# Block input tables of an S5 layer loaded ahead, one block input a step, scans in more and smaller steps

## The chip, the cores and the metric

One NeuronCore of one Trainium2 chip. The metric is the device time of one launch in microseconds. The kernel before takes 2320.91 us, the median of 3 runs (2318.3 to 2321.55).

## The reference

One inference step of a two-layer streaming encoder on two groups of rows at once: a prompt of 512 frames and a running stream of 64 frames, model width 1024. Layer 0 mixes in time with an S5 state-space mixer, layer 1 with differential attention over shared keys and values. Each layer has two SwiGLU feed-forward blocks around its mixer and a LayerNorm after each of the three.

```python
x = layer_norm(ALPHA * x + 0.5 * swiglu(x, w_in[l, 0], w_out[l, 0]), g[0], b[0])
y = s5_mixer(x, ...) if l < N_A else diff_attention(x, ...)
x = layer_norm(ALPHA * x + y, g[1], b[1])
x = layer_norm(ALPHA * x + 0.5 * swiglu(x, w_in[l, 1], w_out[l, 1]), g[2], b[2])
```

The change touches only the S5 mixer. It is a linear recurrence with complex diagonal states, 64 groups of 64 states, followed by a projection to the outputs:

```python
bu = einsum('gpc,btgc->btgp', bb, u_blk)              # complex, bb from the discretised parameters
hs = associative_scan(h[t] = lam_bar * h[t-1] + bu[t])
y_blk = einsum('gcp,btgp->btgc', c_re, hs_re) - einsum('gcp,btgp->btgc', c_im, hs_im)
y = y_blk + d_skip * u                                # then gelu, w_glu, a gated output
```

## The kernel before

All activations stay on the chip, transposed: 8 tiles of 128 features by 576 columns. The columns are worked in two halves, half 0 with 256 and half 1 with 320 (the last 64 of them the running stream). TensorE goes through one long list of weight tiles, 128 outputs by 8 (or 7) rows of 128 inputs. A tile's weights come in float32 from memory into `raw` (four buffers, issued by SyncE), ScalarE rounds them to `wh` (L509), VectorE writes the remainder `wl` (L515), three buffers each, and TensorE does three matmuls for each row (L537 to L539). A feed-forward block has 68 tiles (60 where its last part is held back), in the order gate tile, inner tile and so on, then output tiles.

Everything else is written as generators that are advanced one step after each tile, on each engine by itself: `together` runs several side by side, `chained` one after the other, `idle(n)` skips n steps, and `paced(work, n)` gives work exactly n steps. Engines meet only at semaphores. `packed(work, room)` puts the instructions of a generator into steps: each instruction reports a size, and a step ends when the sizes reach the room; the excess is taken over to the next.

The S5 mixer of a half runs beside a feed-forward block of the other half: `dve_s5`, `act_s5`, `pe_s5` and `pool_s5` of half 0 beside block (0, 1), of half 1 beside block (1, 0), each after the 12 steps of a LayerNorm. Its time axis is cut into blocks of 4 frames. Its steps, counted from 0 at its own start, are these:

- Steps 0 to 5: VectorE and ScalarE rearrange the inputs into `u4` (L1491).
- Block inputs, 8 of them (`dt`): `pe_s5` multiplies `u4` by a table `wt2` of 512 KB (L1711), dt at step 4 + 2 dt, into two banks of `misc` that alternate; ScalarE copies the result into `hs` a step later (L1633), and issues the load of table dt + 2 into the buffer that was just read, as there are two buffers. On every second dt it also issues the loads of an output table `cp2` (512 KB) and `tt2` (256 KB), which have four buffers.
- Two scans, one for each group of four dt, on VectorE alone: `dve_scan` goes up and down a tree over the blocks (L1533 to L1544) with 56 instructions (half 0) or 61 (half 1), of which the widest have 1024 or 1280 elements a partition. `SCAN` is the number of steps of a scan, 11 and 15 for the two halves, and `SCAN_ROOM` its room, 1800 and 1620. The first scan begins at step 11, the second SCAN steps later.
- Outputs: `outputs_at(h, grp)` is the step at which TensorE waits for the scan of a group and begins its four output steps (L1728 and L1731): 23 and 34 for half 0, 27 and 42 for half 1. Four steps later VectorE (L1496) and ScalarE copy them out, and ScalarE applies the GELU.

At the very end the last norm of half 1 is worked out on VectorE in rows and stored by SyncE (L2591). TensorE, which has nothing left to do then, runs the 90 matmuls of `FILL` (L2920 to L2924) on old data into a bank that nobody reads.

Of the kernel before, what the change touches and what calls it, by code (L numbers as in the profile page):

```python
# [15 lines left out]
P = 128  # L16
D = 1024
DT = D // P
# [70 lines left out]
def _ffn(f, h, held=False):  # L89

    for p in range(len(PARTS)):
# [39 lines left out]
BUSY_NORMS = {(0, 1): 10, (2, 1): 5, (3, 1): 4}  # L131
FILL = ((256, 0, 0), (320, 0, 0), (288, 0, 0), (512, 0, 0), (384, 0, 0), (320, 32, 0), (288, 32, 0), (320, 4, 0), (304, 0, 0),
        (320, 0, 16), (320, 16, 0), (448, 0, 0), (256, 32, 0), (320, 0, 4), (272, 0, 0), (320, 0, 32), (192, 0, 0), (320, 8, 0))

# [96 lines left out]
def build(nc, x_prompt, x_sample, cache_k, cache_v, state_re, state_im, ln_g, ln_b, w_in, w_out,  # L231
# [4 lines left out]
    with ctx:  # L236

        def sem(name):
            return ctx.enter_context(nc.semaphore(name))
# [1224 lines left out]
        s_u4a = sem("u4_ready_act")  # L1464
        s_wl = [sem(f"wt2_loaded{s}") for s in range(2)]
        s_bl = [sem(f"cp2_tt2_loaded{s}") for s in range(4)]
# [12 lines left out]

        SCAN = (11, 15)  # L1480
        INPUTS = 4

        def outputs_at(h, grp):
            return 12 + (grp + 1) * SCAN[h]

# [105 lines left out]
        def dve_s5(dve, h):  # L1591
            scans = chained(idle(11), paced(packed(dve_scan(dve, h, 0), SCAN_ROOM[h]), SCAN[h]),
                            paced(packed(dve_scan(dve, h, 1), SCAN_ROOM[h]), SCAN[h]))
            return paced(together(dve_u4(dve, h), scans,
                                  chained(idle(outputs_at(h, 0) + 4), dve_y(dve, h, 0)),
                                  chained(idle(outputs_at(h, 1) + 4), dve_y(dve, h, 1))), s5_steps(h))

        SCAN_ROOM = (1800, 1620)

# [11 lines left out]
        def act_load_inputs(act, h, dt):  # L1611
            n = DT * h + dt
            wait(act, s_wm, n - 1)
            act.dma_start(wt2[dt % 2][:].rearrange("p a q s -> p (a q s)"), scr_w[dt]).then_inc(s_wl[dt % 2], 16)

        def act_load_outputs(act, h, dt):
            n = DT * h + dt
            wait(act, s_ym, n - 3)
            act.dma_start(cp2[dt % 4][:].rearrange("p a q n -> p (a q n)"), scr_c[dt]).then_inc(s_bl[dt % 4], 16)
            act.dma_start(tt2[dt % 4][:].rearrange("p q n -> p (q n)"), scr_t[dt]).then_inc(s_bl[dt % 4], 16)  # L1620

        def act_block_inputs(act, h):
            n, G = NBLK[h], NGRP[h]
            tables_stored(act)
            act_load_inputs(act, h, 0)
            act_load_inputs(act, h, 1)
            yield from idle(INPUTS + 1)
            for dt in range(DT):
                act.wait_ge(s_wm, DT * h + dt + 1)
                if dt == 0 and h:  # L1630
                    act.wait_ge(s_ym, DT)
                for ri in range(2):
                    nc.scalar.copy(hs[:, dt // 4, 0:G, 1:GB + 1, ri, 4 * (dt % 4):4 * (dt % 4) + 4],  # L1633
                                   misc[:, 2 * (dt % 2) + ri, 0:4 * n].rearrange("p (q g i) -> p g i q", q=4, i=GB)
                                   ).then_inc(s_wc, 1)
                if dt + 2 < DT:
                    act_load_inputs(act, h, dt + 2)
                yield
                if dt % 2 == 0:
                    act_load_outputs(act, h, dt // 2)  # L1640
                yield
# [53 lines left out]
        def pe_s5(pe, h):  # L1695
            n = NBLK[h]
            yield from idle(INPUTS)
            for dt in range(DT):
                s = dt % 2
                if dt % 4 == 0:  # L1700
                    pe.wait_ge(s_u4d, len(U4_DVE) * (2 * h + dt // 4 + 1))
                    pe.wait_ge(s_u4a, len(U4_ACT) * (2 * h + dt // 4 + 1))
                if dt == 0 and h:
                    pe.wait_ge(s_yd, 2 * len(Y_DVE))
                    pe.wait_ge(s_ya, 2 * len(Y_ACT))
                pe.wait_ge(s_wl[s], 16 * (DT // 2 * h + dt // 2 + 1))
                if dt >= 2:
                    pe.wait_ge(s_wc, 2 * (DT * h + dt - 1))
                for ri in range(2):
                    for q in range(4):  # L1710
                        mm = nc.tensor.matmul(misc[:, 2 * s + ri, q * n:(q + 1) * n], wt2[s][:, ri, q, :],  # L1711
                                              u4[:, dt, q, 0:n], start=True, stop=True, skip_group_check=True)
                mm.then_inc(s_wm, 1)
                yield from idle(2)
            at = INPUTS + 2 * DT
            for grp in range(2):
# [922 lines left out]
        def _(act):  # L2639
# [23 lines left out]
            finish(beside)  # L2663
            beside = chained(act_ln(act, 0, 1), act_s5(act, 1))
            ffn(1, 0, beside)
# [190 lines left out]
        def _(pe):  # L2856
# [62 lines left out]
            finish(beside)  # L2919
            for cols, at, w_at in FILL:  # L2920
                for j in range(5):
                    w, x = wh[j % 2][:].rearrange("p k c -> p (k c)"), (hh, hl)[j % 2][:].rearrange("p k n -> p (k n)")
                    nc.tensor.matmul(ps[:, 0, 0:cols], w[:, w_at:w_at + P], x[:, at:at + cols],  # L2923
                                     start=True, stop=True, skip_group_check=True)  # L2924

# [40 lines left out]
```

## Time and profile before

| | |
|---|---|
| median of 3 runs | 2320.91 us (2318.3 to 2321.55) |
| the profiled execution | 2318.73 us, span of its instructions 2316.9 us |
| TensorE busy, matmuls | 2257.6 us, 97% of the span |
| VectorE busy | 1525.1 us, 66% |
| ScalarE busy | 1144.4 us, 49% |
| GpSimd busy | 575.2 us, 25% |
| loaded from memory | 366.53 MB, 168 GB/s over the span with what is written |
| mean granted TensorE clock | 0.996 |

The span is what the instructions of the profiled execution cover; the time has a little around it. A share is an average over stages, so an engine with 66% can be the one that is late in a stage. PE is TensorE, PEld its weight load, DVE VectorE, ACT ScalarE, POOL GpSimd, SP SyncE, and a q behind the name its queue. A line number of a weight tile is that of a helper, so stages are told apart by their time: the S5 steps of half 0 run from about 285 us, those of half 1 from about 605 us.

### The profile page before, as it was taken

To read this page: it belongs to the slowest core of one execution; us is meant where nothing else is said; L and a number is where in the kernel's file an instruction comes from. 1 tells how busy PE (TensorE), PEld (TensorE's weight loads), DVE (VectorE), ACT (ScalarE), POOL (GpSimd) and SP (SyncE) were. 2 spreads that over 40 slices of the span, in tenths; PEclk is the share of its full clock that TensorE was granted. 3 is DMA by queue.
4 is the path that set the end of the run, shared out by engine and by line. 5 is a ranking of instruction groups with operands and counts; after the bars stand their busy time and mean duration, and the time that the engine had idled before them with its cause. 6 is when DMAs were issued, how large, how long until landed. Compare 5 with 4: busy or idle time off the path is not lost.

```text
span 2316.9 us, 42849 instructions
## 1 busy us (share of the span) xinstructions
PE 2257.6 (97%) x17261; PEld 2217.1 (96%) x17261; DVE 1525.1 (66%) x2292; ACT 1144.4 (49%) x1923; POOL 575.2 (25%) x491
## 2 busy tenths in 40 slices
PE   8989999999998998999999999999999999999999
PEld 8989999999998998999999999999999998999999
DVE  6898768657788578444475575656677665475444
ACT  4434543555645546433365465555466564354332
POOL 2267401123211343111251123010352011132110
PEclk9999999999999999999999999999999999999999
DMA  9568675454765455655569656544556456355452
GB/s 251 168 194 234 191 217 181 123 171 137 218 216 172 138 162 148 183 151 147 151 191 291 189 160 178 154 122 134 148 154 189 135 147 190 115 152 170 143 156 80
DMA packets 705367, 391.15 MB, mean 169 GB/s; under 512 B 25001, under 2 KB 693138, under 8 KB 705170
## 3 DMA queue, kind: packets, MB, share of 16 engines
q1 hardware_dynamic: 662720, 332.44, 49.6%
q10 hardware_dynamic: 42450, 55.96, 7.3%
q8 instruction: 138, 2.26, 0.4%
q14 instruction: 59, 0.48, 0.1%
HBM read 366.53 MB, written 21.82 MB: 168 GB/s over the span
## 4 chain that ended last, share of the span: by engine, by line
PE 75%; DVE 9%; ACT 2%; issue 2%; POOL 1%; ACTq 0%; POOLq 0%; DVEq 0%
PE tile_ps L537 22%; PE tile_ps L539 22%; PE tile_ps L538 22%; DVE wl L515 3%; PE misc L1731 1%; PE misc L1711 1%; ACT wh L509 1%; PE misc L2064 1%; PE misc L2089 1%; POOL zq L870 1%; PE misc L2264 1%; DVE r L828 1%; DVE hs L1539 1%; PE tile_ps L2923 1%; PE misc L1728 1%
## 5 line engine op out<-in xcount | busy, mean ns | idle before, releaser
L515 DVE TENSOR_TENSOR wl<-raw,wh 128x1024 fp32r<-128x1024 f32 (+1 forms) x640 | 796.6, 1245 | 444.2 <-ACT wh L509 442.3
L537 PE MATMUL tile_ps<-xh,wh 128*128 128x256 f32 (+1 forms) x3520 | 1051.9, 299 | 21.4 <-DVE wl L515 16.9
L539 PE MATMUL tile_ps<-xh,wl 128*128 128x256 f32 (+1 forms) x3520 | 1035.5, 294 | 0.0
L538 PE MATMUL tile_ps<-xl,wh 128*128 128x256 f32 (+1 forms) x3520 | 1035.4, 294 | 0.0
L509 ACT CAST wh<-raw 128x1024 fp32r<-128x1024 f32 (+1 forms) x640 | 655.0, 1025 | 734.0 <-PE tile_ps L539 723.3
L537 PEld LDWEIGHTS tile_ps<-xh,wh 128*128 128x128 f32 x3520 | 666.1, 189 | 29.5 <-issue 18.7
L538 PEld LDWEIGHTS tile_ps<-xl,wh 128*128 128x128 f32 x3520 | 666.1, 189 | 0.9
L539 PEld LDWEIGHTS tile_ps<-xh,wl 128*128 128x128 f32 x3520 | 665.9, 189 | 0.0
L725 POOL TENSOR_TENSOR hl<-hf,hh 128x256 fp32r<-128x256 f32 (+1 forms) x176 | 243.7, 1384 | 1269.8 <-ACT hh L633 1269.2
L537 PE MATMUL tile_ps<-hh,wh 128*128 128x320 f32 (+1 forms) x1472 | 441.9, 300 | 5.4 <-DVE wl L515 5.1
L538 PE MATMUL tile_ps<-hl,wh 128*128 128x320 f32 (+1 forms) x1472 | 433.0, 294 | 0.0
L539 PE MATMUL tile_ps<-hh,wl 128*128 128x320 f32 (+1 forms) x1472 | 432.8, 294 | 0.0
L537 PEld LDWEIGHTS tile_ps<-hh,wh 128*128 128x128 f32 x1472 | 276.9, 188 | 9.5 <-issue 7.5
L538 PEld LDWEIGHTS tile_ps<-hl,wh 128*128 128x128 f32 x1472 | 277.0, 188 | 0.3
L539 PEld LDWEIGHTS tile_ps<-hh,wl 128*128 128x128 f32 x1472 | 276.8, 188 | 0.0
L698 DVE SCALAR_TENSOR_TENSOR r<-r,tile_ps 128x256 f32<-128x256 f32 (+1 forms) x208 | 94.0, 452 | 142.8 <-PE tile_ps L539 141.5
L627 ACT ACTIVATE sil<-tile_ps 128x320 f32<-128x320 f32 (+1 forms) x140 | 57.6, 412 | 179.6 <-PE tile_ps L539 177.8
L675 DVE SCALAR_TENSOR_TENSOR hf<-sil,tile_ps 128x256 f32<-128x256 f32 (+1 forms) x176 | 79.4, 451 | 79.3 <-PE tile_ps L539 77.0
L633 ACT CAST hh<-hf 128x256 fp32r<-128x256 f32 (+1 forms) x176 | 75.7, 430 | 69.8 <-DVE hf L675 68.2
L764 POOL TENSOR_TENSOR zc<-zc,r 128x256 f32<-128x256 f32 (+1 forms) x64 | 65.3, 1020 | 123.3 <-DVE r L698 76.5
L890 POOL TENSOR_TENSOR xl<-r,xh 128x256 fp32r<-128x256 f32 (+1 forms) x60 | 68.8, 1165 | 91.3 <-ACT xh L803 52.6
L870 POOL TENSOR_TENSOR zq<-zq,sq 128x256 f32<-128x256 f32 (+1 forms) x54 | 61.7, 1142 | 17.5 <-ACT sq L798 11.6
(303 smaller groups left out, 1803.4 us busy)
## 6 DMA issues: line engine op xcount, KB each, us to landing
raw<-in_ffn_w_in_dram SPq DMA_DIRECT2D x352, 512.0 KB, 3.8
raw<-in_ffn_w_out_dram SPq DMA_DIRECT2D x128, 448.0 KB, 3.7
raw<-in_ffn_w_out_dram SPq DMA_DIRECT2D x64, 512.0 KB, 4.0
raw<-in_ssm_w_glu_dram SPq DMA_DIRECT2D x32, 512.0 KB, 3.8
raw<-in_attn_w_kv_dram SPq DMA_DIRECT2D x32, 512.0 KB, 4.0
wt<-scr_w ACTq DMA_DIRECT2D x16, 512.0 KB, 4.7
cp<-scr_c ACTq DMA_DIRECT2D x16, 512.0 KB, 4.3
raw<-in_attn_w_q_dram SPq DMA_DIRECT2D x16, 512.0 KB, 3.9
```

What stands on the lines that cost most here:

```text
L509: nc.scalar.copy(wh[n % WS][:, 0:k, :], raw[n % RAWS][:, 0:k, :]).then_inc(w_hi, 1)
L515: nc.vector.tensor_tensor(wl[n % WS][:, 0:k, :], raw[n % RAWS][:, 0:k, :], wh[n % WS][:, 0:k, :].bitcast(F32), ALU.subtract).then_inc(w_lo, 1)
L537: nc.tensor.matmul(o, wh[w][:, kk, :], xa, start=kk == 0, stop=False)
L538: nc.tensor.matmul(o, wh[w][:, kk, :], xb, start=False, stop=False)
L539: return nc.tensor.matmul(o, wl[w][:, kk, :], xa, start=False, stop=kk == ROWS[n] - 1)
L633: nc.scalar.copy(hh[:, i, 0:N], hf[:, 0:N]).then_inc(hh_ready, 1)
L675: nc.vector.scalar_tensor_tensor(out=hf[:, 0:N], in0=sil[:, 0:N], scalar=0.25 if (f, h, p) in TANH else 0.5, in1=bank(n + 1, h), op0=ALU.m ...
L698: nc.vector.scalar_tensor_tensor(out=r[:, d, CS[h]], in0=r[:, d, CS[h]], scalar=alpha, in1=bank(n, h), op0=ALU.mult, op1=ALU.add).then_inc ...
L725: nc.gpsimd.tensor_tensor(hl[:, i, 0:N], hf[:, 0:N], hh[:, i, 0:N].bitcast(F32), ALU.subtract).then_inc(hl_ready, 1)
L764: nc.gpsimd.tensor_tensor(zc[:, 0:N], zc[:, 0:N], r[:, d, CS[h]], ALU.add).then_inc(ln_zc, 1)
L870: nc.gpsimd.tensor_tensor(zq[:, 0:N], zq[:, 0:N], sq[d % 3][:, 0:N], ALU.add).then_inc(ln_zq, 1)
L890: nc.gpsimd.tensor_tensor(low[:, d, 0:NT[h]], r[:, d, CS[h]], high[:, d, 0:NT[h]].bitcast(F32), ALU.subtract).then_inc(x_ready[h], 1)
```

## The change

1. Six block input tables are on chip at a time instead of two: two in `wt2` and four in the buffers of the output tables `cp2`, which have the same size (`input_table`). In half 0 they are loaded in steps 0 to 4, in half 1 in the first steps of the feed-forward block before the norm (`act_inputs_ahead`). Tables 6 and 7 go into `wt2` once block inputs 0 and 1 are multiplied.
2. A block input is multiplied in each step from 4 to 11, instead of in every second one from 4 to 18.
3. The output tables of group 0 are loaded at steps 13, 15, 17 and 19, once the buffers are free of input tables.
4. The scans begin at step 8 instead of 11, and have 13 and 12 steps in half 0, 17 and 16 in half 1, with rooms of 1490, 1620, 1400 and 1490. `outputs_at` gives 22 and 34 for half 0, 26 and 42 for half 1. The S5 work has as many steps in all as before, 47 and 55.
5. The `FILL` matmuls at the end are left out.

```diff
--- before.py
+++ after.py
@@ -129,8 +129,6 @@
 BUSY_TILES = {FIRST["in", 3, 1, 0]: 5}
 BUSY_ROWS = {FIRST["in", 1, 0, 0]: 4, FIRST["o", 1]: 8}
 BUSY_NORMS = {(0, 1): 10, (2, 1): 5, (3, 1): 4}
-FILL = ((256, 0, 0), (320, 0, 0), (288, 0, 0), (512, 0, 0), (384, 0, 0), (320, 32, 0), (288, 32, 0), (320, 4, 0), (304, 0, 0),
-        (320, 0, 16), (320, 16, 0), (448, 0, 0), (256, 32, 0), (320, 0, 4), (272, 0, 0), (320, 0, 32), (192, 0, 0), (320, 8, 0))
 
 HID = {}
 for _f in range(4):
@@ -1462,7 +1460,7 @@
 
         s_u4d = sem("u4_ready_dve")
         s_u4a = sem("u4_ready_act")
-        s_wl = [sem(f"wt2_loaded{s}") for s in range(2)]
+        s_wl = [sem(f"block_input_table_loaded{b}") for b in range(6)]
         s_bl = [sem(f"cp2_tt2_loaded{s}") for s in range(4)]
         s_wm = sem("block_inputs_multiplied")
         s_wc = sem("block_inputs_copied")
@@ -1477,11 +1475,17 @@
         s_so = sem("states_copied")
 
 
-        SCAN = (11, 15)
+        SCAN = ((13, 12), (17, 16))
         INPUTS = 4
+        SCAN_AT = INPUTS + 4
 
         def outputs_at(h, grp):
-            return 12 + (grp + 1) * SCAN[h]
+            return SCAN_AT + 1 + sum(SCAN[h][:grp + 1])
+
+        def input_table(h, dt):
+            b = dt % 6
+            table = wt2[b] if b < 2 else cp2[b - 2]
+            return table, s_wl[b], 16 * (2 * h + 1 + dt // 6 if b < 2 else h + 1)
 
         def s5_steps(h):
             return outputs_at(h, 1) + 13
@@ -1589,13 +1593,13 @@
                 yield
 
         def dve_s5(dve, h):
-            scans = chained(idle(11), paced(packed(dve_scan(dve, h, 0), SCAN_ROOM[h]), SCAN[h]),
-                            paced(packed(dve_scan(dve, h, 1), SCAN_ROOM[h]), SCAN[h]))
+            scans = chained(idle(SCAN_AT), paced(packed(dve_scan(dve, h, 0), SCAN_ROOM[h][0]), SCAN[h][0]),
+                            paced(packed(dve_scan(dve, h, 1), SCAN_ROOM[h][1]), SCAN[h][1]))
             return paced(together(dve_u4(dve, h), scans,
                                   chained(idle(outputs_at(h, 0) + 4), dve_y(dve, h, 0)),
                                   chained(idle(outputs_at(h, 1) + 4), dve_y(dve, h, 1))), s5_steps(h))
 
-        SCAN_ROOM = (1800, 1620)
+        SCAN_ROOM = ((1490, 1620), (1400, 1490))
 
         def act_u4(act, h):
             tables_stored(act)
@@ -1609,22 +1613,28 @@
                         yield
 
         def act_load_inputs(act, h, dt):
-            n = DT * h + dt
-            wait(act, s_wm, n - 1)
-            act.dma_start(wt2[dt % 2][:].rearrange("p a q s -> p (a q s)"), scr_w[dt]).then_inc(s_wl[dt % 2], 16)
+            table, loaded, _ = input_table(h, dt)
+            wait(act, s_wm, DT * h + dt - 5 if dt >= 6 else DT * h)
+            wait(act, s_ym, DT * h)
+            act.dma_start(table[:].rearrange("p a q s -> p (a q s)"), scr_w[dt]).then_inc(loaded, 16)
 
         def act_load_outputs(act, h, dt):
             n = DT * h + dt
+            act.wait_ge(s_wm, DT * h + min(dt + 3, DT))
             wait(act, s_ym, n - 3)
             act.dma_start(cp2[dt % 4][:].rearrange("p a q n -> p (a q n)"), scr_c[dt]).then_inc(s_bl[dt % 4], 16)
             act.dma_start(tt2[dt % 4][:].rearrange("p q n -> p (q n)"), scr_t[dt]).then_inc(s_bl[dt % 4], 16)
 
         def act_block_inputs(act, h):
             n, G = NBLK[h], NGRP[h]
-            tables_stored(act)
-            act_load_inputs(act, h, 0)
-            act_load_inputs(act, h, 1)
-            yield from idle(INPUTS + 1)
+            if h == 0:
+                tables_stored(act)
+                act_load_inputs(act, h, 0)
+                for dt in range(1, INPUTS + 2):
+                    act_load_inputs(act, h, dt)
+                    yield
+            else:
+                yield from idle(INPUTS + 1)
             for dt in range(DT):
                 act.wait_ge(s_wm, DT * h + dt + 1)
                 if dt == 0 and h:
@@ -1633,11 +1643,18 @@
                     nc.scalar.copy(hs[:, dt // 4, 0:G, 1:GB + 1, ri, 4 * (dt % 4):4 * (dt % 4) + 4],
                                    misc[:, 2 * (dt % 2) + ri, 0:4 * n].rearrange("p (q g i) -> p g i q", q=4, i=GB)
                                    ).then_inc(s_wc, 1)
-                if dt + 2 < DT:
-                    act_load_inputs(act, h, dt + 2)
-                yield
-                if dt % 2 == 0:
-                    act_load_outputs(act, h, dt // 2)
+                if dt < 2:
+                    act_load_inputs(act, h, dt + 6)
+                yield
+            for dt in range(4):
+                act_load_outputs(act, h, dt)
+                yield
+                yield
+
+        def act_inputs_ahead(act):
+            for dt in range(6):
+                act_load_inputs(act, 1, dt)
+                yield
                 yield
 
         def act_y(act, h, grp):
@@ -1697,22 +1714,23 @@
             yield from idle(INPUTS)
             for dt in range(DT):
                 s = dt % 2
+                table, loaded, count = input_table(h, dt)
                 if dt % 4 == 0:
                     pe.wait_ge(s_u4d, len(U4_DVE) * (2 * h + dt // 4 + 1))
                     pe.wait_ge(s_u4a, len(U4_ACT) * (2 * h + dt // 4 + 1))
                 if dt == 0 and h:
                     pe.wait_ge(s_yd, 2 * len(Y_DVE))
                     pe.wait_ge(s_ya, 2 * len(Y_ACT))
-                pe.wait_ge(s_wl[s], 16 * (DT // 2 * h + dt // 2 + 1))
+                pe.wait_ge(loaded, count)
                 if dt >= 2:
                     pe.wait_ge(s_wc, 2 * (DT * h + dt - 1))
                 for ri in range(2):
                     for q in range(4):
-                        mm = nc.tensor.matmul(misc[:, 2 * s + ri, q * n:(q + 1) * n], wt2[s][:, ri, q, :],
+                        mm = nc.tensor.matmul(misc[:, 2 * s + ri, q * n:(q + 1) * n], table[:, ri, q, :],
                                               u4[:, dt, q, 0:n], start=True, stop=True, skip_group_check=True)
                 mm.then_inc(s_wm, 1)
-                yield from idle(2)
-            at = INPUTS + 2 * DT
+                yield
+            at = INPUTS + DT
             for grp in range(2):
                 yield from idle(outputs_at(h, grp) - at)
                 at = outputs_at(h, grp) + 4
@@ -2661,7 +2679,7 @@
             beside = act_ln_quick(act, 1, 0)
             act_out(act, 0, 1, 2, beside)
             finish(beside)
-            beside = chained(act_ln(act, 0, 1), act_s5(act, 1))
+            beside = together(act_inputs_ahead(act), chained(act_ln(act, 0, 1), act_s5(act, 1)))
             ffn(1, 0, beside)
             finish(beside)
             act.dma_start(cosT[:, :], rope_cos).then_inc(s_cs, 16)
@@ -2917,11 +2935,6 @@
             beside = together(chained(pe_ln(pe, 5, 0), pe_y_a(pe)), chained(idle(Y_LAST + 2), pe_y_b(pe)))
             ffn(3, 1, beside)
             finish(beside)
-            for cols, at, w_at in FILL:
-                for j in range(5):
-                    w, x = wh[j % 2][:].rearrange("p k c -> p (k c)"), (hh, hl)[j % 2][:].rearrange("p k n -> p (k n)")
-                    nc.tensor.matmul(ps[:, 0, 0:cols], w[:, w_at:w_at + P], x[:, at:at + cols],
-                                     start=True, stop=True, skip_group_check=True)
 
 
 def rope_tables():
```

## Rows read from the trace of the kernel before

**Rows 1.** The page: busy time by engine, and the chain that ended last by line.

```profile
PE 2257.6 (97%) x17261; PEld 2217.1 (96%) x17261; DVE 1525.1 (66%) x2292; ACT 1144.4 (49%) x1923; POOL 575.2 (25%) x491
...
PE tile_ps L537 22%; PE tile_ps L539 22%; PE tile_ps L538 22%; DVE wl L515 3%; PE misc L1731 1%; PE misc L1711 1%; ACT wh L509 1%; PE misc L2064 1%; PE misc L2089 1%; POOL zq L870 1%; PE misc L2264 1%; DVE r L828 1%; DVE hs L1539 1%; PE tile_ps L2923 1%; PE misc L1728 1%
```

**Rows 2.** Waits of TensorE, 370 to 435 us: in total, times, longest.

```profile
PE tile_ps L537 <- DVE wl L515: 2.0, 2, 1.4
PE misc L1728 <- DVE hs L1544: 1.7, 1, 1.7
```

**Rows 3.** Waits of TensorE, 640 to 700 us.

```profile
PE tile_ps L537 <- DVE wl L515: 1.1, 2, 0.9
PE misc L1728 <- DVE hs L1544: 0.6, 1, 0.6
```

**Rows 4.** Waits of TensorE, 700 to 765 us.

```profile
PE tile_ps L537 <- DVE wl L515: 7.0, 5, 2.7
PE misc L1728 <- DVE hs L1544: 0.4, 1, 0.4
```

**Rows 5.** Stretches: length, busy PE, PEld, DVE, ACT, POOL (counts), clock, DMA share, GB/s.

```profile
626.70:646.70 20.00, 20.00 (x173) 20.00 (x173) 9.38 (x12) 7.19 (x11) 0.00 (x0) 1.00 0.89 272
646.70:699.10 52.40, 50.64 (x429) 49.87 (x427) 50.16 (x91) 22.54 (x38) 9.01 (x7) 1.00 0.63 201
699.10:721.20 22.10, 22.05 (x182) 22.05 (x183) 17.07 (x23) 3.30 (x4) 0.00 (x0) 1.00 0.77 238
721.20:761.40 40.20, 33.13 (x252) 32.10 (x251) 38.35 (x75) 26.60 (x36) 9.86 (x7) 0.92 0.47 138
```

**Rows 6.** Timeline of VectorE: start, us, operation [idle before it, releaser].

```profile
638.13 1.23 DVE L515 TENSOR_TENSOR wl<-raw,wh 128x1024 fp32r<-128x1024 f32 x1 [0.71 <-ACT wh L509]
...
647.07 1.49 DVE L1533 TENSOR_TENSOR sa<-hs,lam 128x1280 f32<-128x1280 f32 x1
648.48 0.82 DVE L1535 TENSOR_TENSOR sb<-hs,lam 128x640 f32<-128x640 f32 x1
...
650.68 0.82 DVE L1537 TENSOR_TENSOR sb<-hs,lam 128x640 f32<-128x640 f32 x1
651.53 1.49 DVE L1539 TENSOR_TENSOR hs<-hs,sa 128x1280 f32<-128x1280 f32 x1
653.06 0.42 DVE L698 SCALAR_TENSOR_TENSOR r<-r,tile_ps 128x256 f32<-128x256 f32 x1
653.40 1.22 DVE L515 TENSOR_TENSOR wl<-raw,wh 128x1024 fp32r<-128x1024 f32 x1
654.53 2.02 DVE L1542 TENSOR_TENSOR hs<-hs,sb 128x1280 f32<-128x1280 f32 x1
```

**Rows 7.** Timeline of TensorE around two block inputs and the first outputs.

```profile
624.74 1.91 PE L1711 MATMUL misc<-u,wt 128*128 128x80 f32 x16
626.44 0.36 PE L537 MATMUL tile_ps<-hh,wh 128*128 128x256 f32 x1
...
632.18 1.91 PE L1711 MATMUL misc<-u,wt 128*128 128x80 f32 x16
...
699.15 0.45 PE L1728 MATMUL misc<-u,tt 128*128 128x80 f32 x2 [0.61 <-DVE hs L1544]
```

**Rows 8.** The end: closing matmuls (ns min/median/max), VectorE's last row, its stores.

```profile
L2923 PE MATMUL tile_ps<-hh,wh x54: 250/308/393, 2302.1 to 2315.3; 128*128 128x320 f32 x24, 128*128 128x256 f32 x6, 128*128 128x288 f32 x6, 128*128 128x512 f32 x3
...
2312.11 1.28 DVE L2575 SCALAR_TENSOR_TENSOR yrow<-yrow,ysd,brow 64x1024 f32<-64x1024 f32 x1
...
out_dram<-yrow SPq DMA_DIRECT2D x1, 256.0 KB, 2.9
```

**Rows 9.** The page, DMA issues: KB each, median us from issue to landing.

```profile
wt<-scr_w ACTq DMA_DIRECT2D x16, 512.0 KB, 4.7
```

**Rows 10.** Stretches: length, busy PE, granted clock, DMA share, GB/s.

```profile
734.00:735.00 1.00, 0.99 (x9) 1.00 1.02 301
738.00:742.00 4.00, 4.00 (x24) 0.57 0.47 131
```

## The prediction, made before the changed kernel ran

> **What bounds the kernel now.** I read the page first. TensorE is busy for 97% of the span, and the chain that ended last is the three matmul lines of the weight tiles, 22% each [rows 1]. So time can be won or lost only where TensorE waits, and where instructions are added to or taken from it. Then I read the waits of TensorE alone in the three stretches that the change touches. While the S5 work of half 0 runs, TensorE waits 2.0 us for weight remainders (`wl`, written by VectorE) and 1.7 us for a finished scan [rows 2]: 3.7 us. For the first scan of half 1 it is 1.1 + 0.6 us [rows 3], for the second 7.0 + 0.4 us [rows 4]: 9.1 us. All of it is VectorE being late; no wait for a table load stands in these answers. The stretches by engine say why: from 646.7 to 699.1 VectorE is busy 50.16 of 52.40 us, from 721.2 to 761.4 38.35 of 40.20, but from 626.7 to 646.7, while the first block inputs are multiplied, only 9.38 of 20.00 [rows 5]. So the bound in these stages is VectorE, and the question is what the new step plan does to the moment at which each scan ends and to the moment at which TensorE asks for it.
>
> **Numbers of one step (half 1).** A weight tile of 8 rows takes (632.18 - 624.74 - 1.70)/2 = 2.87 us on TensorE, 1.70 being the 16 matmuls of a block input: the next weight matmul starts that long after the first of them [rows 7]; a tile of 7 rows 7/8 of it, 2.51. VectorE owes each step 0.34 us (residual add, start to start) and 1.13 us (`wl`), 1.48 together [rows 6], 1.34 with 7 rows. Scan instructions, start to start: 1280 elements 1.41 us, 1.53 when linked to the one before; 640 elements linked 0.85; in general elements/960 + 0.08, or + 0.20 if linked. About one in two steps loses a further 0.53 us: the third 1280-element row starts after a `wl` and takes 2.02 where its twin takes 1.49 [rows 6].
>
> **Scan packing, from the code.** A scan of half 1 has 61 instructions with sizes that sum to 23,740. Room 1620 packs them into 14 batches: 2040, 2040, 1340, 1080, 1780, 1580, 1496, 1804, 1540, 1840, 1780, 1340, 1400, 2680. They start at S5 step 11, so the last falls on step 24 of 11 to 25, and TensorE asks at step 27. Room 1400 makes 17 batches: 2040, 2040, 1340, 700, 1460, 1080, 1200, 1372, ..., the last 1340 on step 24 of 8 to 24; TensorE asks at step 26. Group 1: before 26 to 39, asked at 42; after 16 batches (room 1490) on 25 to 40, asked at 42. So three earlier steps are gained at the front, yet the last batch has the same VectorE step (24) or a later one (39 to 40), and its margin to the asking step falls from three steps to two. The totals of steps do not change (47 and 55), nor does any instruction of the S5 work.
>
> **Group 0 of half 1.** VectorE does the same work up to the end of step 24 in both kernels, so the scan ends later or sooner only by the difference in VectorE's idle time. Before: 10.6 us idle in 626.7 to 646.7, and of the 2.24 us not busy until 699.1 I take 1.0 as waits, the rest as gaps between instructions: 11.6 [rows 5]. After: each of the steps 4 to 11 carries a block input, 2.87 + 1.70 = 4.57 us of TensorE. The tile of step 6 ends 1.70 later than now, at 626.44; the `wl` of step 8 is done 2 x 4.57 + 2.26 after it (0.42 + 0.71 wait for ScalarE + 1.13 [rows 6]), at 637.8. From 626.4 that is 11.4 us less three steps of 1.48: 7.0 idle. Steps 8 to 11 give VectorE 4 x 4.57 = 18.3 us for 4 x 1.48 and four batches, 2.5 + 2.4 + 1.5 + 0.75 = 7.2: 5.2 idle. Sum 12.2 against 11.6, so the scan ends where it does now, +-1 us. But it is asked for one tile earlier. Now TensorE has finished the tile of step 27 at 698.5 and waits 0.6; after, it has that tile still to do when the scan ends, and waits instead. It is one tile behind: **+2.9 us** (bounds +1.5 and +4). Where a stall goes, the later one takes its place: the waits for `wl` shrink or grow, the sum to that point is VectorE's.
>
> **Group 1 of half 1.** Before, VectorE has caught up at 721.2 (step 31) and is then full to the scan's end at 761.4, 40.2 us [rows 5]. After, it catches up last at step 30, because the four output steps, 22.1 us for four tiles [rows 5], now lie at 26 to 29. From there it owes the same plus two steps' own work (1.34 + 1.34, steps 30 and 40) and 700 elements of size that were done earlier before (0.75 us): 3.4 us more, from a start 2.51 us sooner. VectorE's four `ysb` copies lie one step earlier and inside both sums. **+0.9 us** (bounds 0 and +2).
>
> **Half 0.** FFN columns are 320 here, tiles longer, margins to the asking step two and two in both kernels (last batches at 21/32 asked at 23/34; after 20/32, asked at 22/34). What changes is group 1: by step 27 the sizes done sum to 11,592 against 10,900, so about 690 elements, 0.7 us, less remain behind the same deadline. **-0.7 us** of the 3.7 waited (bounds -2 and 0). The final batches (1656, 1656, 1084) are the same, so the 1.7 us wait for the scan stays.
>
> **Loads and queues.** The same 48 loads move the same bytes. In half 1 six input tables move to steps 0 to 10 of the feed-forward ahead, past the first norm; ScalarE's instructions behind them wait for nothing, as the counts that they ask for (all block inputs and outputs of half 0) were reached a stage before. In half 0 six tables of 512 KB in five steps of 3.5 us stand beside one weight tile of 512 KB each: 11 x 0.524 MB in 17.7 us, 326 GB/s, above the 301 GB/s of a full microsecond [rows 10]. The excess, 0.4 MB, is 1.5 us of queue. A table lands in 4.7 us [rows 9] and is issued three steps, 10 us, before it is multiplied; a weight tile is issued some three tiles ahead. Hidden: 0, and up to +3 if not. The Trainium skill ("DMA: Bandwidth & Descriptors", on issuing engines not being separate DMA queues) says that loads issued by different engines run on the same 16 engines and interleave, which speaks against bunching them; taken alone it would put the 1.5 us into the weight tiles' landing, which the sum leaves hidden. Output tables of 4 dts are issued at steps 13 to 19 instead of 6 to 18 and are needed from 22 or 26: hidden. Block inputs in successive steps need ScalarE's two copies within one step of 4.57 us, beside 1.05 of cast: hidden.
>
> **The 90 closing matmuls.** They run from 2302.1 to 2315.6 and write a buffer that nobody reads [rows 8]. They look like the end of the chain [rows 1], but VectorE's last row goes to 2313.4 and its store takes 2.9 us more, 2316.3 of a span of 2316.9 [rows 8]. The store is the cover: the end moves by 0 (bounds -0.7 and 0).
>
> **The sum.** +2.9 + 0.9 - 0.7 + 0 = +3.1 us on the profiled execution's 2318.73 (span 2316.9 and 1.8 around it): 2321.8. The median of the runs shown is 2320.91, 2.2 us above it; on it the forecast is 2324.0.
>
> **Rivals.** (A) The lighter steps do relieve VectorE: 1400 to 1490 of size per step are 0.14 to 0.23 us less than 1620, over 12 steps 2 to 3 us that TensorE would not wait, and if the idle time at the front is really used, most of the 12.8 us goes, with the slow clock in it: -6, 2315. For it: three more steps. Against it: the packing above, whose sizes done by steps 35 to 38 are equal to the unit (16,540 to 21,060), and 12.2 us idle that stays. 0.14. (B) Slower by more: the new waits sit together ahead of an output step and the clock falls over it. Now the granted clock is 1.00 before the two waits of 2.7 and 2.0 us in 735 to 751 but 0.57 over 738 to 742, a fall to 1.2 GHz after the first, which is 4 x 0.43 = 1.7 us of work lost [rows 10]; there most of it is hidden, since VectorE binds. After group 0 of half 1 nothing hides it: the four output steps are TensorE's. One such there, and one later beside another norm, give +3.1 + 1.7 + 1.7 = +6.5, 2327.4. It decides once TensorE's wait at the asking step reaches about the 2.7 us seen. The Trainium skill ("TensorE: Matmul & The Clock Gate", Part 1) calls the gate free-running, not reset by the kernel; by that, which waits are hit would vary from run to run, and the same plan could give +3 or +6. 0.26. (C) The step plan is shifted but nothing is late enough to matter, within 1 us of now: 2321.5. This lies inside my range and shares its class. 0.10.
>
> **Numbers.** The forecast has 0.50. A measurement of this kernel can tell about 0.2% (4.6 us) from no change, so +3.1 is within it. Same: most of the forecast and of C, and a little of A and B: 0.59. Slower: most of B and the upper end of the forecast (+4.6 is 1.5 above it): 0.27. Faster: A, 0.14. Range: from -4 (the low half of A left out) to +7.5: 2317 to 2328.5.
>
> **What would show it.** Right: the wait of the first output matmul of half 1 for its scan grows from 0.6 us towards 2, the waits before it sum to about 4 with it instead of 1.7; those of the second scan to about 8; the scan of group 0 ends at the same distance from the last `u4` copy; half 0 loses under 1 us of its 3.7; VectorE stays near half idle in steps 6 to 8; the end is a store. Wrong: VectorE busy through the block inputs, waits under 5 us in half 1, a wait for `wh` on a load, or a span that shrinks by the closing matmuls.

## The result, and the profile after

The changed kernel takes 2329.82 us, the median of 6 runs (2326.86 to 2331.74), against 2320.93 (2318.3 to 2322.8): a ratio of 1.0037, 95% interval 1.0027 to 1.0047. It is slower, where the forecast was 2324.0 with a change too small to tell from none. The profiled execution took 2331.31 us, in the upper part of its kernel's runs, with a span of 2329.5; that is 12.6 us over the one of before, so its pieces add up to more than the 8.9 us between the medians.

The page of the changed kernel, busy time and the chain that ended last (compare [rows 1]; the lines have moved by two, L535 to L537 are the weight tiles, and L1746 and L1749 the output matmuls):

```profile
PE 2252.4 (97%) x17171; PEld 2210.4 (95%) x17171; DVE 1524.7 (65%) x2292; ACT 1144.0 (49%) x1923; POOL 573.7 (25%) x491
...
PE 71%; DVE 8%; issue 6%; POOL 3%; ACT 2%; ACTq 0%; POOLq 0%; DVEq 0%
```

TensorE is busy 5 us less, as the closing matmuls are gone, yet the span grew. The kernel before without its closing matmuls (the first run below) is busy for 2242.5 us with the same 17171 instructions: so the same matmuls took 9.9 us longer here. The waits of TensorE (total us, times, longest), first for 370 to 435 us, then 640 to 706, then 706 to 775, answer to [rows 2 to 4]:

```profile
PE misc L1746 <- DVE hs L1548: 2.1, 1, 2.1
PE tile_ps L535 <- DVE wl L513: 2.0, 3, 1.0
...
PE tile_ps L535 <- DVE wl L513: 2.1, 3, 1.1
PE misc L1746 <- DVE hs L1548: 1.8, 1, 1.8
...
PE tile_ps L535 <- DVE wl L513: 7.0, 5, 2.1
PE misc L1746 <- DVE hs L1548: 0.6, 1, 0.6
```

Half 0 waits 4.1 us (3.7 before), half 1 11.5 (9.1): +2.8 us of waits. That is close to what the forecast said of the sum of waits, +3.1. Most of the rest stands in the granted clock. Stretches of the changed kernel (length, busy of PE, PEld, DVE, ACT and POOL, clock, DMA share, GB/s):

```profile
626.00:646.00 20.00, 20.00 (x176) 20.00 (x176) 12.62 (x22) 10.08 (x17) 0.00 (x0) 1.00 0.62 186
646.00:705.30 59.30, 55.23 (x464) 53.82 (x463) 53.08 (x93) 25.23 (x40) 7.78 (x7) 1.00 0.65 194
433.60:443.80 10.20, 10.20 (x46) 10.20 (x45) 2.52 (x3) 0.00 (x0) 0.00 (x0) 0.52 0.50 143
706.70:713.50 6.80, 6.80 (x35) 6.80 (x34) 5.73 (x9) 0.00 (x0) 0.00 (x0) 0.53 0.48 137
```

And the same place in half 0 of the kernel before:

```profile
433.00:444.00 11.00, 11.00 (x87) 11.00 (x86) 3.07 (x4) 3.36 (x5) 1.82 (x2) 1.00 0.50 144
```

TensorE is busy in both, but gets through 46 instructions in 10.2 us where it got through 87 in 11.0: 1.2 GHz instead of 2.4. Right ahead of each slow stretch it had waited for a scan, as the timeline of TensorE shows (start, us, idle before in brackets). The third line is of the weight tile behind the first output step of half 0: it runs slow as well.

```profile
433.11 0.62 PE L1746 MATMUL misc<-u,tt 128*128 128x64 f32 x2 [2.08 <-DVE hs L1548]
433.52 1.06 PE L1749 MATMUL misc<-hs,cp 128*128 128x64 f32 x4
...
439.13 0.47 PE L535 MATMUL tile_ps<-hh,wh 128*128 128x320 f32 x1
...
705.25 0.45 PE L1746 MATMUL misc<-u,tt 128*128 128x80 f32 x2 [1.77 <-DVE hs L1548]
```

At these two places 10.2 x 0.48 = 4.9 and 6.8 x 0.47 = 3.2 us of work were lost; the kernel before lost nothing at either (1.00 in the line above, and 1.00 over 699.10 to 721.20 in [rows 5]). By landmarks (the same matmul in both traces), the profiled executions differ by 1.4 us before the S5 steps begin, by 0.6 more at the first output of the second scan of half 0, by 4.8 more at the norm after that stage, by 5.4 more at the second scan of half 1, and by 0.4 more in all that follows. The 1.4 us is there before any changed step runs, and nothing here explains it; in other profiles below this difference is up to 4.3 us. At the end VectorE and the store still close the kernel:

```profile
2322.30 4.21 SPq L2609 DMA_DIRECT2D out_dram<-yrow  x3
...
2324.69 1.28 DVE L2593 SCALAR_TENSOR_TENSOR yrow<-yrow,ysd,brow 64x1024 f32<-64x1024 f32 x1
```

### The profile page after: what moved, and what is told of

The parts are those of the page before. It is cut to its first block, busy times and chain, and to the rows that moved or that the text cites. A ratio compares the mean times of both kernels' runs of the same rounds, so it can differ in the third digit from the quotient of the medians.

```text
span 2329.5 us, 42689 instructions
## 1 busy us (share of the span) xinstructions
PE 2252.4 (97%) x17171; PEld 2210.4 (95%) x17171; DVE 1524.7 (65%) x2292; ACT 1144.0 (49%) x1923; POOL 573.7 (25%) x491
## 4 chain that ended last, share of the span: by engine, by line
PE 71%; DVE 8%; issue 6%; POOL 3%; ACT 2%; ACTq 0%; POOLq 0%; DVEq 0%
PE tile_ps L535 21%; PE tile_ps L537 21%; PE tile_ps L536 21%; DVE wl L513 2%; PE misc L1749 2%; POOL zq L868 1%; PE misc L2082 1%; ACT wh L507 1%; PE misc L2107 1%; POOL hl L723 1%; PE misc L2282 1%; PE misc L1746 1%; PE misc L1729 1%; DVE r L826 1%; DVE hs L1543 0%
## 5 line engine op out<-in xcount | busy, mean ns | idle before, releaser
L535 PE MATMUL tile_ps<-xh,wh 128*128 128x256 f32 (+1 forms) x3520 | 1052.3, 299 | 22.0 <-DVE wl L513 17.0
L537 PE MATMUL tile_ps<-xh,wl 128*128 128x256 f32 (+1 forms) x3520 | 1035.1, 294 | 0.0
L535 PEld LDWEIGHTS tile_ps<-xh,wh 128*128 128x128 f32 x3520 | 665.5, 189 | 31.6 <-issue 19.0
L537 PEld LDWEIGHTS tile_ps<-xh,wl 128*128 128x128 f32 x3520 | 665.1, 189 | 0.0
L535 PE MATMUL tile_ps<-hh,wh 128*128 128x320 f32 (+1 forms) x1472 | 443.5, 301 | 5.7 <-DVE wl L513 5.6
L537 PE MATMUL tile_ps<-hh,wl 128*128 128x320 f32 (+1 forms) x1472 | 434.0, 295 | 0.0
L535 PEld LDWEIGHTS tile_ps<-hh,wh 128*128 128x128 f32 x1472 | 278.0, 189 | 10.0 <-issue 8.0
L537 PEld LDWEIGHTS tile_ps<-hh,wl 128*128 128x128 f32 x1472 | 277.7, 189 | 0.0
L868 POOL TENSOR_TENSOR zq<-zq,sq 128x256 f32<-128x256 f32 (+1 forms) x54 | 62.8, 1163 | 17.4 <-ACT sq L796 11.5
```

Source lines behind the costliest of these rows:

```text
L535: nc.tensor.matmul(o, wh[w][:, kk, :], xa, start=kk == 0, stop=False)
L537: return nc.tensor.matmul(o, wl[w][:, kk, :], xa, start=False, stop=kk == ROWS[n] - 1)
L868: nc.gpsimd.tensor_tensor(zq[:, 0:N], zq[:, 0:N], sq[d % 3][:, 0:N], ALU.add).then_inc(ln_zq, 1)
```

## The experiments

The theory: TensorE's waits grow by about 3 us, and the waits of 1.8 and 2.1 us stand just ahead of the output steps, over which the clock then falls. Rivals: waits alone, the loads, the closing matmuls.

**The parts one by one.** The closing matmuls alone:

```diff
-            for cols, at, w_at in FILL:
-                for j in range(5):
...
```

> The kernel before without the 90 closing matmuls and nothing else. Theory 'scans and clock' (the 8.9 us come from the S5 steps): the end is VectorE's last row and its store, so the time stays within 1 us of the kernel before (2320.9). Rival 'closing matmuls' (they matter for a reason that the trace does not show): some of the 8.9 us shows here, 2323 or more, and the span starts or ends otherwise.

2319.7 us, ratio 0.9998 (0.9989 to 1.0006), span 2316.9 as before. The rival is out, and every run below whose edit starts from the changed kernel can be read against the kernel before.

This profile shows one thing more. Its S5 steps are those of the kernel before, yet TensorE waits 10.5 us in half 1, not 9.1. The stretch where the difference arises, first before, then without the closing matmuls:

```profile
750.00:757.00 7.00, 6.11 (x39) 6.14 (x40) 6.96 (x6) 2.93 (x6) 5.10 (x3) 0.76 0.42 124
...
750.00:757.00 7.00, 5.22 (x43) 5.08 (x44) 6.96 (x6) 3.04 (x6) 5.11 (x3) 1.00 0.41 119
```

VectorE is full in both. Where the clock fell, TensorE worked slower and waited less; where it did not, it waited instead. So in the stretch that VectorE bounds a slow clock costs next to nothing, and sums of waits in half 1 can be compared only between profiles with as many slow stretches there. The kernel before and the changed one have two each.

Then the tables ahead and one block input a step, with the old steps for everything else:

```diff
-        SCAN = ((13, 12), (17, 16))
+        SCAN = ((11, 11), (15, 15))
+        OUTPUTS = ((23, 34), (27, 42))
...
-        SCAN_AT = INPUTS + 4
+        SCAN_AT = (11, 11)
...
-            return SCAN_AT + 1 + sum(SCAN[h][:grp + 1])
+            return OUTPUTS[h][grp]
...
-        SCAN_ROOM = ((1490, 1620), (1400, 1490))
+        SCAN_ROOM = ((1800, 1800), (1620, 1620))
```

> Tables loaded ahead and one block input a step, without the closing matmuls, but both scans and the outputs at the steps and rooms of the kernel before (start 11; 11, 11, 15, 15 steps; outputs at 23, 34, 27, 42). Theory 'scans and clock': 2320 to 2323, as no scan moves; waits before the outputs as in the kernel before (1.7, 0.6, 0.4 us), no half clock over the output steps. Rival 'loads' (bunched tables delay weight tiles, or one input a step takes VectorE's time from the first scan): a wait of ScalarE for a load, or 2326 and more.

2331.91 us, 1.0052 (1.0039 to 1.0064): at least as slow as the whole change, whose interval (1.0027 to 1.0047) it overlaps. My theory was that nothing would happen without a moved scan; it is wrong. Waits of TensorE in 370 to 440 us and in 640 to 780, and the stretch behind a new wait of 1.5 us at the first outputs of half 0:

```profile
PE misc L1747 <- DVE hs L1549: 3.2, 2, 1.7
PE tile_ps L535 <- DVE wl L513: 2.0, 2, 1.4
...
PE tile_ps L535 <- DVE wl L513: 15.0, 13, 2.7
PE misc L1747 <- DVE hs L1549: 0.9, 2, 0.6
...
384.70:391.50 6.80, 6.80 (x35) 6.80 (x36) 6.73 (x8) 0.46 (x1) 1.29 (x1) 0.58 0.45 124
```

No wait of TensorE or of ScalarE in these stages is for a load. Whether it is the loads' place or the block inputs' was settled by putting the block inputs back to every second step, and with them ScalarE's copies and the loads of the output tables between them:

```diff
-            for dt in range(4):
-                act_load_outputs(act, h, dt)
-                yield
+                if 2 <= dt < 6:
+                    act_load_outputs(act, h, dt - 2)
...
-                yield
-            at = INPUTS + DT
+                yield from idle(2)
+            at = INPUTS + 2 * DT
```

> Tables loaded ahead, but block inputs in every second step and the scans and outputs as in the kernel before; no closing matmuls. The run with one input a step had 2331.9. Theory 'block inputs leave the first scan' (four of the eight, 6.8 us of TensorE, stood beside the first scan of each half and gave VectorE time): 2319 to 2322, no wait before the first outputs of half 0. Rival 'loads': 2326 or more, as the loads are where they were.

2322.95 us, 1.0000 (0.9991 to 1.0009), 1 us above what the theory gave and far from the rival's 2326, and the waits of half 0 are those of before, with no wait at its first outputs:

```profile
PE tile_ps L535 <- DVE wl L513: 2.0, 2, 1.4
PE misc L1746 <- DVE hs L1549: 1.7, 1, 1.7
...
PE tile_ps L535 <- DVE wl L513: 8.1, 7, 2.6
PE misc L1746 <- DVE hs L1549: 0.8, 2, 0.5
```

So loading the input tables ahead costs and brings nothing. One block input a step, with the copies and output tables that go with it, costs 9 us between the medians of these two runs and 12 by their ratios. The theory names the reason: four of the eight used to stand beside the first scan and gave VectorE 4 x 1.7 us there. The waits fit it: 15.9 us in half 1 against 8.9 with the old block input steps, of which some 3 us stand for two slow stretches that only the second of these profiles has. The 1.7 us beside each step were not varied by themselves. Then, on top of the run with one input a step, the scan steps of one half at a time:

> As the run before, with the changed kernel's scan steps in half 0 alone. Theory 'scans and clock': TensorE's waits change by under 1 us, but the wait for the second scan is about 2.1 us and the granted clock then falls to half over the output steps, 10 us long in the profile of the changed kernel: 2325 to 2327 where it falls. Rival 'waits alone': 2320 to 2322.

> As the second run, with the changed kernel's scan steps in half 1 alone. Theory 'scans and clock': the first scan is asked for one tile earlier, +2 to +3 us by waits, and +3.4 us where the clock falls over its output steps (6.8 us at half): 2323 to 2327. Rival 'waits alone': 2323 to 2324 and the clock at 1.0 over the outputs of group 0.

2327.80 us, 1.0030 (1.0019 to 1.0041), with the new scans of half 0 alone, 2329.62, 1.0044 (1.0030 to 1.0058), with those of half 1 alone. Both lie above what the theory gave, which had counted from about 2321, while the run that they start from took 2331.91. The waits show what each repairs of what one input a step had broken: 4.1 us in half 0 instead of 5.2, and 11.2 in half 1 instead of 15.9, or of 13.0 in the first of the two, which has the same steps there and as many slow stretches. Between the times only the gain of the first is clear of noise, and just so. And the fall of the clock that the theory expected came in neither profile: none behind the wait of 2.1 us at the second outputs of half 0 in the first, none behind the 1.85 us at the first outputs of half 1 in the second. So a wait of that length does not always bring the clock down. The intervals overlap with the changed kernel's, and I do not rank them.

**The clock.** Spare matmuls keep TensorE busy until the scan is there:

```diff
+        BUSY_SCANS = ((0, 9), (8, 3))
...
-                pe.wait_ge(s_sh, 2 * h + grp + 1)
                 pe.wait_ge(s_wc, 2 * DT * (h + 1))
...
+                pe_busy(misc[:, 0, 0:P], BUSY_SCANS[h][grp])
+                pe.wait_ge(s_sh, 2 * h + grp + 1)
```

> The changed kernel, with TensorE kept busy by 9 spare matmuls of ones before it waits for the second scan of half 0, 8 before the first and 3 before the second scan of half 1; they end about when the scan does. Theory 'scans and clock': the granted clock stays at 1.0 over the output steps, which gives back up to the 5.1 and 3.4 us that the profile lost there: 2322 to 2326. Rival 'waits alone': no gain, 2329 to 2331.

2323.87 us, 1.0010 (1.0001 to 1.0018): 6 us less than the changed kernel. The spare matmuls on the timeline of TensorE, and the stretches that were slow (PE alone, then clock):

```profile
431.94 2.17 PE L524 MATMUL misc<-vec,ones 128*128 128x128 f32 x18
434.17 0.43 PE L1749 MATMUL misc<-u,tt 128*128 128x64 f32 x2
...
430.00:446.00 16.00, 15.94 (x125) 1.00 0.57 162
697.00:712.00 15.00, 15.00 (x125) 1.00 0.58 178
```

No work was saved, and VectorE is as late as it was (2.0 and 9.2 us of waits for `wl` against 2.0 and 9.1 in the changed kernel; the waits for the scans are filled by the spare matmuls). Only the clock held at these two places. What is left over the kernel before, 2.5 us, is the waits' share.

The other way round, the kernel before with its second scan of half 0 made later:

```diff
                 else:
+                    if h == 0 and grp == 1:
+                        link(dve, V.tensor_tensor(t1[..., halves[0]], cur[..., halves[1]], lim[..., halves[0]], ALU.mult))
                     V.tensor_tensor(nxt, nxt, t1, ALU.add).then_inc(done, 1)
```

> The kernel before, with the second scan of half 0 made about 0.7 us later by one 512-element product that is done twice with the same result. Theory 'clock': TensorE's wait for that scan goes from 1.7 to about 2.3 us, above the 2.1 of the changed kernel, and the granted clock then often falls over the four output steps, for 3.4 to 10 us: 2323 to 2327. Rival 'waits alone': +0.7, 2321 to 2322.

and with `link(dve, V.tensor_tensor(t0, cur, lre, ALU.mult))` ahead of it as well:

> The same with that scan about 2.0 us later (a 1024-element product as well). Theory 'clock': the wait is about 3.6 us and the clock falls in nearly every run: +2.0 by the wait and +3 to +5 by the clock, 2326 to 2329. Rival 'waits alone': +2.0, 2323.

2324.15 us, 1.0019 (1.0010 to 1.0028), and 2326.83 us, 1.0024 (1.0014 to 1.0033). First the one, then the other, the first output matmul and the stretch behind it:

```profile
433.94 0.43 PE L1730 MATMUL misc<-u,tt 128*128 128x64 f32 x2 [2.79 <-DVE hs L1546]
...
434.00:446.00 12.00, 12.00 (x72) 12.00 (x73) 4.80 (x6) 2.69 (x3) 1.79 (x2) 0.72 0.33 93
```

```profile
436.87 0.48 PE L1731 MATMUL misc<-u,tt 128*128 128x64 f32 x1 [4.46 <-DVE hs L1547]
...
434.50:446.00 11.50, 9.13 (x39) 9.13 (x40) 5.35 (x6) 0.00 (x0) 1.24 (x2) 0.60 0.40 118
```

The waits grew by 1.1 and 2.8 us, more than the 0.7 and 2.0 that I had expected, and the times by 3.6 and 6.3 between the medians (4.4 and 5.6 by the ratios). In both the clock fell behind the wait: 12.0 x 0.28 = 3.4 us of work in the first, three times what the wait had grown by, and 11.5 x 0.40 = 4.6 us in the second, where the wait is 4.46.

**Where the outputs are asked for.** The changed kernel with one step more before the first outputs of half 1:

```diff
+        OUTPUTS = ((22, 34), (27, 42))
...
-            return SCAN_AT + 1 + sum(SCAN[h][:grp + 1])
+            return OUTPUTS[h][grp]
```

> The changed kernel with TensorE asking for the first scan of half 1 at step 27 again instead of 26, nothing else. Theory 'asked a tile earlier': the 1.8 us wait before the first output shrinks to under 0.5 and the clock does not fall over these outputs: 2 to 5 us less than the changed kernel, 2325 to 2328. Rival 'VectorE's order alone' (the sum of the waits is VectorE's and does not care where they stand): within 1 us of 2329.8.

2324.81 us, 1.0012 (1.0003 to 1.0020), 5 us less than the changed kernel, as the theory had it (its range began at 2325). There is no wait before these outputs any more. But the waits of half 1 (640 to 780 us) hardly shrank:

```profile
PE tile_ps L535 <- DVE wl L513: 9.7, 10, 1.9
PE misc L1747 <- DVE hs L1549: 1.4, 1, 1.4
```

11.1 us against 11.5 (all idle time of TensorE there, 11.7 in both): what the first scan no longer costs, waits beside the second one do. A part of that is the clock's: it falls once in the stretch that VectorE bounds, not twice as in the changed kernel, and by the first run a fall there takes 1.4 us off the waits. The gain in time is a scan wait gone from ahead of the first outputs, where in this profile the clock no longer falls (1.00 over 700 to 714 us).

**A version that beats both.** Scans from step 8 as in the change, but with room before each asking step:

```diff
-        SCAN = ((13, 12), (17, 16))
+        SCAN = ((14, 11), (20, 12))
+        OUTPUTS = ((26, 34), (32, 42))
...
-            return SCAN_AT + 1 + sum(SCAN[h][:grp + 1])
+            return OUTPUTS[h][grp]
...
-        SCAN_ROOM = ((1490, 1620), (1400, 1490))
+        SCAN_ROOM = ((1400, 1800), (1300, 1900))
```

> Tables ahead and one input a step, scans from step 8, but 14 and 11 steps in half 0 with outputs at 26 and 34, 20 and 12 in half 1 with outputs at 32 and 42, rooms 1400, 1800, 1300, 1900: four to seven steps between the last batch of the first scan and its outputs. Adding up VectorE's steps by the durations of the trace gives no wait in half 0 and 5 us in half 1, against 4.1 and 11.5 in the changed kernel. Theory 'margins': 2311 to 2317. Rival 'VectorE has simply too much to do': over 2320.

2313.84 us, 0.9967 (0.9955 to 0.9979). Waits in 370 to 440 us and 640 to 780:

```profile
PE misc L1747 <- DVE ysb L1501: 1.7, 1, 1.7
...
PE tile_ps L535 <- DVE wl L513: 4.6, 6, 1.2
PE misc L1747 <- DVE hs L1549: 1.2, 1, 1.2
```

The 1.7 us were not in my sum: the copies of the first outputs were late for the second. With the first outputs of half 0 at 25:

> The run with wide margins (2313.8) with the first outputs of half 0 at 25 instead of 26. There TensorE waited 1.7 us at the second outputs of half 0 for the copies of the first ones. Theory 'copies': one step earlier these copies are in time, and the wait falls below 0.5 us: 2311 to 2313. Rival 'the scan takes their place': VectorE's copies, now beside the same scan a step earlier, leave the scan as late as it was: the wait stays above 1 us, 2313 to 2315.

2312.15 us, 0.9964 (0.9951 to 0.9976), within noise of the run before it. The time would fit the theory (2311 to 2313), but the wait decides: the one for the copies is gone, and one of 1.3 us for the scan has taken its place, as the rival said. Last, the kernel before with nothing but its first outputs later:

```diff
-            return 12 + (grp + 1) * SCAN[h]
+            return ((26, 34), (30, 42))[h][grp]
```

> The kernel before with one line changed: TensorE asks for the first scan's outputs at step 26 instead of 23 in half 0, and at 30 instead of 27 in half 1; tables, block inputs, scans and closing matmuls as they were. Theory 'margins' (what pays is where the four output steps and their copies stand beside the second scan, which is VectorE's tightest stretch, not loading ahead): the waits of half 0 fall from 3.7 to under 2 us, those of half 1 from 9 to 6 or 7: 2313 to 2317, most of what the run with wide margins won. Rival 'the early scans are what pays': 2319 or more.

2314.20 us, 0.9970 (0.9959 to 0.9981). One line gives nearly all of it, without any of the change. Waits in 370 to 440 us and 640 to 780:

```profile
PE misc L1728 <- DVE ysb L1496: 1.7, 1, 1.7
...
PE tile_ps L537 <- DVE wl L515: 4.8, 6, 1.5
PE tile_ps L537 <- issue: 1.7, 1, 1.7
PE misc L1728 <- DVE hs L1544: 1.0, 1, 1.0
```

(The 1.7 us put down to "issue" end at 697.95, as VectorE's `wl` of that tile is done at about 697.9, so they look like a wait for VectorE too.) The waits fell by 3.6 us, the time by 6.4; what the rest is was not taken apart.

The likely reason, worked out from the rows and not tested by itself: the four output steps make TensorE's steps some 3 us longer each (22.10 us [rows 5] less four tiles of 2.51). Beside the start of the second scan VectorE could not use that time: its batches are capped by the room, and it idled (17.07 of 22.10 us busy). Three steps later they stand where its lag is greatest.

## Why the prediction was wrong

- **The bound** was read rightly. VectorE's lateness sets these stages; all waits of TensorE in these stages are on it, none on a load (one of 1.7 us, in the last run, is put down to "issue").
- **Scan packing and margins** held: the last batches fell where the code puts them, and the margin, not the start, is what counts.
- **Group 0 of half 1**: the scan ended where the forecast put it. Last `u4` copies and last scan instruction, before and after:

```profile
624.50 1.85 DVE L1491 COPY u<-r 32x320 f32<-32x320 f32 x4
697.18 1.92 DVE L1544 TENSOR_TENSOR hs<-hs,sb 128x1280 f32<-128x1280 f32 x1
...
630.79 1.84 DVE L1495 COPY u<-r 32x320 f32<-32x320 f32 x4
703.71 1.48 DVE L1548 TENSOR_TENSOR hs<-hs,sb 128x1280 f32<-128x1280 f32 x1
```

  From the end of the copies to the end of the scan it is 72.8 us before and 72.6 after. The idle time of VectorE that stays, 12.2 us, is 7.4 in 626 to 646 and at most 6.2 in 646 to 705.3, about as worked out. The price of +2.9 was too high: the waits there grew by 2.2 (1.7 to 3.9). And its reason is shown only in part: asking at 27 again takes the wait away from these outputs and 5 us off the time, but the sum of the waits of half 1 stays at 11.1, partly because the clock fell once less there.
- **Group 1 of half 1**: +0.9 forecast, +0.2 measured (7.4 to 7.6).
- **Half 0**: -0.7 forecast, +0.4 measured. The waits for `wl` stayed at 2.0 and the one for the scan went from 1.7 to 2.1, where I had said that it stays.
- **Loads and closing matmuls**: nothing, measured apart, as forecast. The tables of half 0 landed in 5.6 to 6.6 us instead of 4.7, still in time.
- **The sum of the waits**, +3.1 forecast, was +2.8. That it came so close is partly luck: the two terms of half 1 were too high by 1.4 together, and that of half 0 was too low by 1.1, with the wrong sign.
- **The step that failed** is the sum itself, which has no term for the clock: it adds up waits and puts nothing beside them. In the stretch that I had read the clock's loss is hidden, as VectorE is the bound, and I left it at that. I had it as rival B, at 0.26, for half 1 alone and with a threshold of 2.7 us that I took from the one wait I had looked at. The fall came in half 1 behind a wait of 1.8 us, and in half 0, which B does not name, behind 2.1. The output steps are TensorE's own time, so nothing hides it. It cost 4.9 + 3.2 us in the profile; by the run with spare matmuls, it is 6 us of the 8.9.
- **A price by chance.** The same wait at the second outputs of half 0 had different sequels. A wait of 1.7 us was followed by a full clock in four profiles (the kernel before, without the closing matmuls, tables ahead, first version with wide margins) and by a slow one in three (one input a step, the same with the scans of half 1, the one-line change). A wait of 2.1 us there was followed by a full clock with the scans of half 0 alone, by 3.4 us of slow clock with the outputs of half 1 asked at 27, and by 10.2 us in the changed kernel. The Trainium skill ("TensorE: Matmul & The Clock Gate", Part 1) says that the window in which TensorE's activity is judged runs free and is not reset when a kernel starts. The profiles fit that, though none shows where such a window lies. I had the sentence, and should have drawn from it that such a wait has a price by chance, and not a point from which it decides.

How often the clock falls at each wait stays open, as each kernel has one profile. But every run has its mean granted clock on record, and these bear the account out beyond the profiles. TensorE idles at the end of every kernel without the closing matmuls, and the clock is at 0.50 there, so these are compared with each other. Without the closing matmuls and nothing else the mean is 0.9930 (11 runs), in the changed kernel 0.9898 (6 runs, the highest 0.991), with the spare matmuls 0.9928 (11 runs). The first difference, 0.0032 of 2328 us, is an estimate of 7.4 us of work lost to the clock, hidden losses included; with the 2.8 us of waits it makes 10.2, against 10.1 between the medians. The later scans lower the mean of the kernel before from 0.9950 (21 runs) to 0.9934 and 0.9931, 3.7 and 4.4 us by the same estimate. And the means of single runs of the kernel before go from 0.994 to 0.998, so how much is lost varies from run to run of one kernel.

## What to carry to other kernels

Price a wait of the matrix engine by what follows it, not by its length: 1.1 us more ahead of a stretch that only this engine bounds cost 3.6 here, and whether such a price is paid varies from run to run. Where two engines go in steps, work that makes the one's steps longer is time for the other, so it is worth trying beside the other's fullest steps; look where the other engine stands idle under its own cap before starting it sooner. And run a change's parts apart: here one cost 9 to 12 us, two nothing, and the moved scans gave back some 2 us of it, which is about the size of the noise.

## What the runs showed of the hardware

Behind a wait of 2.1 us TensorE ran at 1.2 GHz for 10.2 us on end though it was busy all that time (10.20 of 10.20 us): half of it over the short float32 matmuls of the output steps, the other half over a whole tile of 320-column ones (0.47 us each instead of 0.31). Behind 1.8 us it was 6.8 us. Spare matmuls of 2.2 us in the first wait itself kept the clock at 1.00. In a stretch that VectorE bounds, one slow stretch more went with 1.4 us fewer waits and no time that the medians show. The 301 GB/s that I took for full [rows 10] are not: with the tables of half 0 bunched, slices of 0.45 us reached 426 GB/s, and no wait of TensorE is for a load.
